# One element-wise step moved between engines in the opening, and two lists of VectorE work reordered

## The reference, cut to what matters

```python
mod = (c_act @ w_ada + b_ada).reshape(bsz, N_MOD, D_MODEL)[:, :, None, :]
u = rms_norm(x, ln1) * (1.0 + scale1) + shift1        # scale1, shift1: from mod
proj = u @ w_in                                        # 1024 -> gates, conv, z, xbc, dt
gl, cb, cc, cx, z, xbc, dt = jnp.split(proj, split_at, axis=-1)
xbc = jax.nn.silu(causal_depthwise_conv(xbc, ssm_conv_w) + ssm_conv_b)
# per group of heads and chunk of tokens:
scores = jnp.einsum('btgn,bsgn->btsg', cq, bq)
y_diag = jnp.einsum('btsg,btsgr,bsgrp->btgrp', scores, decay, xq)
y_off = jnp.einsum('btgn,bgrpn->btgrp', cq, state) * jnp.exp(a_cum)[..., None]
y = (y_diag + y_off + d_skip * xs) * jax.nn.silu(z)    # then a norm per group
```

## Time and profile before

| | us |
|---|---|
| median of 3 runs (1783.82 to 1787.41) | 1784.37 |
| the profiled execution | 1782.47 |
| its span in the trace | 1780.8 |
| PE busy | 1757.5 (99%) |
| DVE busy | 1093.3 (61%) |
| ACT busy | 801.8 (45%) |

### The profile page before, as it was taken

How to read it: one execution, slowest core, us unless ns; L and a number is a source line. 1 busy time by engine, 2 the same in 40 slices (tenths; PEclk the granted TensorE clock), 3 DMA queues, 4 the chain that set the end, 5 groups by cost and what they waited for, 6 DMA issues and landing times.

```text
span 1780.8 us, 25071 instructions
## 1 busy us (share of the span) xinstructions
PE 1757.5 (99%) x8566; PEld 1452.1 (82%) x8566; DVE 1093.3 (61%) x1529; ACT 801.8 (45%) x1157; POOL 239.9 (13%) x312
## 2 busy tenths in 40 slices
PE   7999999999999999999999999999999999999998
PEld 4887777787888888888888888888998888888887
DVE  5787777775346666579855666686656653223343
ACT  4666655565322222365323534664434475125521
POOL 0111111110001110022111126121110200000011
PEclk9999999999999999999999999999999999999999
DMA  9334343332546553336665563111122332332332
GB/s 332 103 121 116 119 119 107 108 117 83 166 142 189 188 188 118 107 97 210 192 192 170 190 224 100 48 49 48 46 74 60 95 95 94 102 99 88 95 101 71
DMA packets 72129, 220.86 MB, mean 124 GB/s; under 512 B 9328, under 2 KB 19952, under 8 KB 72048
## 3 DMA queue, kind: packets, MB, share of 16 engines
q1 hardware_dynamic: 52704, 160.20, 28.8%
q0 software_dynamic: 17632, 56.83, 10.3%
q10 hardware_dynamic: 1712, 2.75, 0.5%
HBM read 217.52 MB, written 2.23 MB: 123 GB/s over the span
## 4 chain that ended last, share of the span: by engine, by line
PE 90%; DVE 5%; DVEq 2%; ACT 2%; DMA 1%; issue 1%; SPq 0%; ACTq 0%
PE bank L406 23%; PE bank L408 23%; PE bank L407 23%; PE bank L1210 2%; PE bank L1212 2%; PE bank L1211 2%; PE bank L437 1%; PE bank L439 1%; PE bank L438 1%; PE bank L1261 1%; PE bank L1262 1%; PE bank L1263 1%; PE bank L628 1%; PE bank L1493 1%; PE bank L632 1%; PE bank L1489 1%
## 5 line engine op out<-in xcount | busy, mean ns | idle before, releaser
L372 ACT ACTIVATE whi<-wraw 128x1024 fp32r<-128x1024 f32 x278 | 293.8, 1058 | 445.1 <-PE bank L408 336.3
L406 PE MATMUL bank<-uhi,whi 128*128 128x512 f32 x1188 | 469.0, 395 | 0.0
L408 PE MATMUL bank<-uhi,wlo 128*128 128x512 f32 x1188 | 462.7, 389 | 0.0
L407 PE MATMUL bank<-ulo,whi 128*128 128x512 f32 x1188 | 462.2, 389 | 0.0
L392 DVE TENSOR_TENSOR wlo<-wraw,whi 128x1024 fp32r<-128x1024 f32 x278 | 342.7, 1234 | 193.3 <-ACT whi L372 174.9
L408 PEld LDWEIGHTS bank<-uhi,wlo 128*128 128x128 f32 x1188 | 223.0, 188 | 47.1
L407 PEld LDWEIGHTS bank<-ulo,whi 128*128 128x128 f32 x1188 | 223.2, 188 | 46.7 <-issue 1.4
L406 PEld LDWEIGHTS bank<-uhi,whi 128*128 128x128 f32 x1188 | 223.1, 188 | 46.5 <-issue 1.4
L406 PE MATMUL bank<-vhi,whi 128*128 128x512 f32 x648 | 252.9, 390 | 0.0
L408 PE MATMUL bank<-vhi,wlo 128*128 128x512 f32 x648 | 252.1, 389 | 0.0
L407 PE MATMUL bank<-vlo,whi 128*128 128x512 f32 x648 | 252.1, 389 | 0.0
(11 more groups left out here) (413 smaller groups left out, 2394.0 us busy)
## 6 DMA issues: line engine op xcount, KB each, us to landing
wraw<-in_units SPq DMA_DIRECT2D x280, 512.0 KB, 3.6
aring<-in_ada POOLq DMA_DIRECT2D x160, 256.0 KB, 3.7
slab<-in_ada SPq DMA_DIRECT2D x32, 256.0 KB, 7.3
es<-decay_rows POOLq DMA_DIRECT2D x32, 256.0 KB, 4.0
eac<-decay_rows POOLq DMA_DIRECT2D x32, 128.0 KB, 3.0
x<-in_xT SPq DMA_DIRECT2D x4, 512.0 KB, 5.9
xr<-in_xT ACTq DMA_DIRECT2D x1, 2048.0 KB, 12.5
outT<-xr SPq DMA_DIRECT2D x12, 128.0 KB, 1.8
```

The lines of the kernel that those rows point to most:

```text
L372: act.activation(whi[:, at % SLOTS, :], wraw[:, at % RAW, :], ACT.Copy).then_inc(w_hi, 1)
L406: pe.matmul(out, wh, rhs_hi(k), start=first and k == 0, stop=False)
L407: pe.matmul(out, wh, rhs_lo(k), start=False, stop=False)
L408: mm = pe.matmul(out, wl, rhs_hi(k), start=False, stop=last and k == KT - 1)
```

## The change

Three edits, all within the first 150 us of the program.

1. In the opening, the rounded part of tile 2 is no longer written by ACT but by DVE, between `modulation(1)` and `scaled_a(3)`. The helper `rounded_a` is what stood there for tile 0, with a drain on both sides.
2. The remainder of the very first weight unit is taken ahead of `columns(1, 0, 1)`, not behind it.
3. In group 2, DVE does slots 0 and 1 and then the remainders of units 3 and 4 of that group, where it did slot 0, both remainders, and then slot 1.

```diff
-                if j > 0:
+                if j not in (0, 2):
                     act.activation(uhi[:, j, :], x0[:, j, :], ACT.Identity, scale=g1s[:, j:j + 1], bias=mod[:, j:j + 1])
...
+            def rounded_a(j):
+                dve.drain()
+                dve.tensor_scalar(uhi[:, j, :], x0[:, j, :], g1s[:, j:j + 1], mod[:, j:j + 1], ALU.mult, ALU.add)
+                dve.drain()
+
...
             modulation(0)
-            dve.drain()
-            dve.tensor_scalar(uhi[:, 0, :], x0[:, 0, :], g1s[:, 0:1], mod[:, 0:1], ALU.mult, ALU.add)
-            dve.drain()
+            rounded_a(0)
             low_a(0)
             scaled_a(1)
+            lo_part(dve, 0, 0)
             columns(1, 0, 1)
-            lo_part(dve, 0, 0)
             low_a(1)
...
             scaled_a(2)
             modulation(1)
+            rounded_a(2)
             scaled_a(3)
...
-            dve_slot(dve, 0, 2, True, True)
-            split_lo(dve, "ssm2", 0, 0)
+            for n in range(2):
+                dve_slot(dve, n, 2, True, True)
+            for n in range(2):
+                split_lo(dve, "ssm2", 0, n)
             for g in range(2, SSM_GROUPS):
-                for n in range(1 if g == 2 else 0, 7):
+                for n in range(2 if g == 2 else 0, 7):
                     split_lo(dve, f"ssm{g}", 0, n)
                     dve_slot(dve, n, g, True, True)
```

## The result

The changed kernel takes 1788.63 us in the median of 20 runs (1787.01 to 1792.23), the kernel before 1783.38 (20 runs, 1780.99 to 1787.41): a ratio of 1.0029, 95% interval 1.0023 to 1.0035, or 5.2 us more. The profiled executions differ by as much: spans of 1780.8 and 1786.0 us.

The account below looks back on a forecast made before the run. PE, busy 1757.5 of 1780.8 us, was taken to bound the kernel. Opening -0.4, stall -0.17 and +5.15, and clock +2.0 summed to +6.6 us on 1784.37, forecasting 1791.0 us, range 1787.0 to 1794.0.

Parts of the forecast that it names:

- The gate moved with the remainder: Group 2: SP's load of unit 5, gated by unit 3's remainder, is issued 6.8 us later, near 147.06.
- The waits exchanged before unit 3: Group 2: PE's 1.43 us wait becomes 1.26 for unit 3's remainder; unit 3 starts about 147.09, gaining 0.17 us.
- The stall: Group 2: PE waits 5.34 us before `pe_b(1, 3)`, released at 158.25, 4.98 us late, or 3.5 with a 3.5 us landing.
- The landing: Group 2: unit 5's load takes 5.0 us from issue to arrival, with 3.5 kept as the lower end.
- the same neighbours: Unit 5's load: another weight load 1.2 us behind and an `es` load shortly before, as at the old place, hence 5.0 us.
- my row: The profile's landing times for unit 5's load, 5.0 us here and 3.5 at least, preferred to the skill's 3.2 us estimate.
- The clock behind the stall: After the stall: PE at half clock from 158.25 to 162.2, 4.0 us, losing 2.0 us; bounds 0 and 3.25.
- The opening: Opening, both edits there together: 0.4 us gained, bounds 0.3 lost to 0.8 gained.
- (b): Group 2, rival: unit 5's load is not late, so only the opening's -0.4 counts: 1784.0 us, no change; chance 0.08.
- (a): Behind the stall, rival: the clock holds, only the stall counts: +4.6 us, 1789.0; chance 0.32.
- the short landing: Group 2, case within the clock-holds rival: unit 5's load lands in 3.5 us, total 1787.5; chance 0.04.
- Sum: Whole kernel: -0.4 opening, -0.17 and +5.15 stall, +2.0 clock, +6.6 us on 1784.37, giving 1791.0.

Follow-up runs that it names:

- the spare buffer: Changed kernel with unit 5 of group 2 loaded into a spare buffer, gated by unit 3's rounding instead of its remainder: 1782.63 us, ratio 0.9993 to the kernel before.
- edit 3 alone: Kernel before with only group 2's slots 0 and 1 put ahead of the two remainders: 1791.32 us against 1784.40, ratio 1.0038.
- the filled stall: Changed kernel with 16 needless 128x512 matmuls on PE between unit 3 of group 2 and `pe_b(1, 3)`: 1787.27 us against 1784.06, ratio 1.0019.
- the opening's edits: Changed kernel with group 2's order on DVE taken back, so only the two changes in the opening stay: 1782.91 us, ratio 0.9997 to the kernel before.
- edit 2: Kernel before with only unit 0's remainder moved ahead of a column: 1782.15 us, ratio 0.9989.
- edit 1: Kernel before with only tile 2's rounded part moved from ACT to DVE: 1783.63 us, ratio 0.9993.
- one remainder behind slot 1: Changed kernel with group 2's order on DVE as slot 0, remainder of unit 3, slot 1, remainder of unit 4: 1784.12 us, ratio 1.0000 to the kernel before.
- the first four experiments: Edit 3 alone, the opening's edits, one remainder behind slot 1, and the spare buffer; the kernel before has a median of 1784.40 us in 30 runs beside them.

## Why the prediction was right, and where its sizes were off

- *The gate moved with the remainder.* Right: load at 147.34 for the 147.06 forecast, and the spare buffer shows that it alone makes the stall.
- *The waits exchanged before unit 3.* Right: 1.43 us gone, 0.96 for `wlo` in its place, unit 3 at 147.36 for 147.09. I had 1.26, by the starts of instructions; the trace counts idle time from the modelled end of the last matmul.
- *The stall.* The landing was mis-sized: 5.0 us forecast from the old place, 3.5 measured, the lower end. That is not the chance of one trace: with the load at its late place the landings are 3.5, 3.8 (edit 3 alone) and 4.0 us (the filled stall), and at the early place 4.9, 5.1, 5.0 and 5.0 (before, the opening's edits, edit 2, edit 1), or 4.4 with one remainder behind slot 1, where the next weight load does not follow. So "the same neighbours" did not hold. So `pe_b(1, 3)` came 3.82 us late, 0.2 to 0.3 of it from the opening, not 4.98. The estimate of 3.2 us that the prediction worked out from the Trainium skill ("DMA: Bandwidth & Descriptors", "Anatomy of one DMA") was nearer to this landing than my row; to the 4.9 and 5.0 of before it was not. What makes it shorter I can't say: the `es` load that I held for the cause was issued 0.29 us ahead of this one too (147.05), and 1.2 us ahead of the slow one.
- *The clock behind the stall.* A fall came and was priced about right, 3.4 us at half and 1.57 us lost by the landmarks (5.39 - 3.82), where I took 4.0 and 2.0. But its course was not the forecast one, and that the sizes agree is in part luck. I had the fall 2.5 us into the stall and 6.8 us long, with 4.0 of them behind the restart. The clock fell at 158.4, 1.3 us behind the restart, and was back at 161.8. In the trace of edit 3 alone it went as I had worked it out, 2.7 us into the stall and 6.8 us long, and 5.2 us of PE's work were at half. Nor are the 2.5 us a constant: in the ten traces the opening's idle time of PE is 2.7 to 3.1 us long, and the fall comes from 0 to 2.5 us after it began. One row of the opening was too little to time this by.
- *The opening.* Up to 46 us it gained 0.75 us, within my bounds, by edit 2 and with the wait at `reduced(2)` gone as said. I forecast 0.4 left; a fall of the clock that no rival held took 1.4 us on the way (from -1.07 to +0.30); it is in seven of the ten traces, edit 3 alone included, and so belongs to the profiled pair and not to the edits. By the runs the opening's edits leave -0.5 us with an interval of 3.6.
- *The rivals.* (b), that the load is not late, and its estimate of no change is what the spare buffer measures once the load is made early. (a) fell with the profile: the clock did not hold. The time alone would have spoken for (a): the measured 1788.63 lies nearer to its 1789.0 than to the 1791.0 forecast, since a shorter landing and a cheaper fall took off what (a) took off by leaving the fall out. The lower end of the range was also ill explained: 1787.0 lies below (a) with the short landing, 1787.5, and not only below (a) with "a landing a little under 5.0".
- *Sum.* 6.6 us forecast; less 1.5 for the landing and 0.4 for the clock, plus 0.7 for the opening (0.3 lost where I had 0.4 gained), is 5.4, the difference at PE's landmark of 165.40. Of the 2.4 us between 1791.0 and 1788.63, the other 1.0 is the starting point: 1784.37 was the median of three runs, and that of 20 is 1783.38.

## What to carry to other kernels

A step that produces data for one engine may also free a buffer, and the queue that waits for the buffer isn't in its order list: before moving a step back, ask what its semaphore opens, and follow that transfer to the next use. Two waits for an engine that has no gap between them are one amount of work, and reordering it moves idle time from one wait to the other: 1.43 + 0.19 us before, 0.24 + 1.35 with one remainder behind slot 1, 0.99 + 0.38 with both behind it and the spare buffer. And a stall of PE can cost more than its own length: the two of 4.0 and 4.3 us here came with 3.4 and 6.8 us at half clock, the waits of 1.4 us and less in group 2 with none.

## What the runs showed of the hardware that I had not expected

The granted clock fell with no idle time of PE ahead. In seven of the ten traces it was at half for 3.4 us between 52 and 62 us, from among the last of the 24 matmuls of 128x1 on that stand there between those of 128x512 (in the changed kernel 16 at 49.54 and 8 at 52.03, and the fall at 52.6); in the traces of before, of the spare buffer and of the filled stall it was not, with the same instructions of PE there. No run here takes these small matmuls away, so that they cause the fall is not shown. The opening's fall also has such matmuls ahead of it, and with edit 1 alone it comes at 20.1 us, as PE's idle time begins (23.26 - 3.09 = 20.17).

The spread of the runs is the clock's as well. The 30 runs of the kernel before that go with the first four experiments lie between 1781.2 and 1788.7 us; the twelve up to 1782.4 have a mean clock of 0.997, those from 1783.9 to 1785.3 have 0.995, and those above 1787 have 0.992 to 0.994. A difference of 0.005 over 1781 us is 2 x 0.005 x 1781 = 18 us more at half clock; the opening of edit 3 alone, 20.5 us at half where before has 6.8, shows that such amounts occur. A single execution of this kernel says little of an edit worth under 6 us, unless its clock is read beside it.
